# Rotation of queries and keys on GpSimd in a decoder layer's second projection pass, with twelve more expert dot products beside it

## What is computed

```python
def rope_partial(x, pos):                       # the first 16 of 64 columns of each head
    cos = jnp.cos(ang)[:, None, :]; sin = jnp.sin(ang)[:, None, :]
    x1, x2 = xr[..., :8], xr[..., 8:16]
    rot = jnp.concatenate([x1 * cos - x2 * sin, x2 * cos + x1 * sin], axis=-1)

def mix_projection(h, w_in, ln_g, ln_b, pos):   # h @ w_in -> u, vn, q, k, v
    q = rope_partial(q, pos) * (HEAD_DIM ** -0.5)
    k = rope_partial(k, pos)

# x += W_out [ gmlp_chunk(u, vn) || dilated window attention(q, k, v) ]
# x += peer_ffn(RMSNorm(x)):
    g = jax.nn.softmax(top_s, axis=-1)          # 8 heads x 16 experts of 16384 for each token
    hid = jax.nn.gelu(jnp.einsum('thkd,td->thk', u_tab[eid], xb))
    return jnp.einsum('thk,thkd->td', g * hid, v_tab[eid])
# y = RMSNorm(x)
```

## Time and profile before

| | us |
|---|---|
| median of 3 runs | 1731.89 |
| the runs | 1735.63, 1730.67, 1731.89 |
| span of the profiled execution | 1733.9 |

### The profile page before, as it was taken

One profiled execution on the slowest core, in us unless ns is written; L12 is line 12 of the kernel. 1 busy time (PEld: TensorE's weight loads), 2 busy tenths in 40 slices (PEclk: granted clock), 3 DMA queues, 4 the chain that ended last, 5 costly groups with the idle time before them and its releaser, 6 DMA issues.

```text
span 1733.9 us, 17751 instructions
## 1 busy us (share of the span) xinstructions
PE 1415.3 (82%) x5140; PEld 625.2 (36%) x5140; DVE 1086.9 (63%) x2913; ACT 637.0 (37%) x1905; POOL 654.3 (38%) x703
## 2 busy tenths in 40 slices
PE   6879997878998968888887887777777877777776
PEld 3475664444433333333332232222222322222211
DVE  2238987977200027777766666666667888888554
ACT  2421112455401004434444354444445434444443
POOL 3014434333366643333333333333333433333332
PEclk9889998788899988999999999999999999999999
DMA  9569899999999989999999999999999999999997
GB/s 342 201 263 336 311 325 349 390 395 408 394 366 351 387 322 372 413 418 402 401 421 410 421 410 422 421 421 412 414 415 411 406 422 414 405 421 418 409 391 325
DMA packets 111856, 664.80 MB, mean 383 GB/s; under 512 B 12912, under 2 KB 14176, under 8 KB 52240
## 3 DMA queue, kind: packets, MB, share of 16 engines
q0 software_dynamic: 97824, 571.75, 82.2%
q1 hardware_dynamic: 13936, 91.92, 13.5%
HBM read 658.02 MB, written 5.60 MB: 383 GB/s over the span
## 4 chain that ended last, share of the span: by engine, by line
DMA 37%; PE 31%; issue 10%; DVE 9%; ACT 8%; another core or an unknown queue 4%; POOL 0%; SPq 0%; ACTq 0%; DVEq 0%; POOLq 0%
DMA area_r<-in_uv_tab,eid 35%; PE bank L822 11%; PE bank L586 6%; PE bank L716 4%; ACT area_c L923 3%; PE bank L766 3%; PE bank L811 3%; DVE area_r L1563 2%; DMA area_w<-in_w_in 1%; PE bank L529 1%; DVE area_r L1554 1%; DVE area_x L1571 1%; PE bank L675 1%; ACT L1150 1%
## 5 line engine op out<-in xcount | busy, mean ns | idle before, releaser
L822 PE MATMUL bank<-area_r,area_c 128*128 128x512 f32 (+1 forms) x1584 | 776.6, 621 | 217.0 <-ACT area_c L923 211.4
L1726 POOL DMA_INDIRECT area_r<-in_uv_tab,eid x544 | 516.5, 949 | 967.3 <-PE bank L822 593.1
L1563 DVE CUSTOM_DVE_ANT_0 area_r<-area_r,bank 128x1024 f32<-128x1024 f32 x416 | 506.1, 1217 | 288.5 <-DMA area_r<-in_uv_tab,eid 287.8
L822 PEld LDWEIGHTS bank<-area_r,area_c 128*128 128x128 f32 (+1 forms) x1584 | 271.8, 187 | 715.4 <-issue 714.8
L1150 ACT ACTIVATE area_c<-hid 128x1 f32<-128x1 f32 x416 | 84.1, 202 | 539.4 <-DVE hid L1563 538.8
L1554 DVE CUSTOM_DVE_ANT_0 area_r<-area_r,bank 128x1024 f32<-128x1024 f32 x128 | 153.2, 1212 | 26.5 <-DMA area_r<-in_uv_tab,eid 26.0
L586 PE MATMUL bank<-area_w,area_t 128*128 128x384 f32 (+1 forms) x448 | 157.2, 507 | 6.2 <-DMA area_w<-in_w_in 5.6
L923 ACT ACTIVATE area_c<-ident,area_c 128x128 f32<-128x128 f32 x364 | 146.1, 401 | 34.8 <-PE bank L822 1.1
L1726 POOL DMA_INDIRECT area_r<-in_uv_tab,eidT x128 | 122.3, 955 | 92.2 <-issue 30.5
L766 PE MATMUL bank<-area_t,area_w 128*128 128x128 f32 (+1 forms) x512 | 129.6, 410 | 8.6 <-ACT area_x L923 7.9
L923 ACT ACTIVATE area_x<-bank 128x384 f32<-128x384 f32 (+8 forms) x125 | 50.3, 424 | 206.2 <-remote 65.5
(11 more groups left out here) (180 smaller groups left out, 1185.2 us busy)
## 6 DMA issues: line engine op xcount, KB each, us to landing
area_w<-in_w_in SPq DMA_DIRECT2D x12, 1536.0 KB, 8.9
area_w<-in_w_q SPq DMA_DIRECT2D x16, 1024.0 KB, 6.8
area_w<-in_k_cache SPq DMA_DIRECT2D x8, 1920.0 KB
area_r<-in_uv_tab,eid POOLq DMA_INDIRECT x544
area_w<-in_w_out SPq DMA_DIRECT2D x4, 2048.0 KB, 12.5
area_w<-in_v_cache SPq DMA_DIRECT2D x4, 1920.0 KB
area_v<-in_v_cache SPq DMA_DIRECT2D x4, 1152.0 KB
area_w<-in_w_in SPq DMA_DIRECT2D x2, 2048.0 KB, 12.7
```

What stands on the lines that cost most here:

```text
L822: mm = pe.matmul(acc[0:n, c, :], diag[by_pe(i) % DG][:, 0:n], x_ring[s][:, D + c * 512:D + (c + 1) * 512], start=(i == 0), stop=False, ski ...
L1563: vec.tensor_tensor_reduce(out=u, in0=u, in1=x_cur, scale=1.0, scalar=0.0, op0=ALU.mult, op1=ALU.add, accum_out=hid[t % 2][:, j:j + 1]).th ...
L1726: nc.gpsimd.indirect_dma_start(out=ring[s], out_offset=None, in_=table, in_offset=bass.IndirectOffsetOnAxis(ap=where, axis=0)).then_inc(la ...
```

## The change

In the second pass GpSimd does the rotations, with the same four operations; the first pass's stay on VectorE. GpSimd's queue is written out by unit: ahead of the rotation of unit u stand the fetches of tile 0 that `gathers_before(u)` allows. These are those whose slots are set free by the dot products made through unit u - 1, so dot products so far plus six, and no more than 16 for each head whose indices are made by then. The rotation waits for `proj_read` and, between its products and its sum, for a semaphore of its own (`rope_scaled`). 88 instead of 76 dot products stand ahead of and beside the pass, and a query or key unit weighs 8 instead of 6 in spreading them.

```diff
-DOTS_FIRST, DOTS_PROJ = 12, 76
+DOTS_FIRST, DOTS_PROJ = 12, 88
+        rope_scaled = sem("rope_scaled")
-        ROOM = [1 if t == SAMP else {"uv": 10, "q": 6, "k": 6, "v": 8}[CHUNKS[c][0]] for c, t in UNITS[NC:]]
+        ROOM = [1 if t == SAMP else {"uv": 10, "q": 8, "k": 8, "v": 8}[CHUNKS[c][0]] for c, t in UNITS[NC:]]
...
-                if UNITS[u] in qk_at:
-                    rotate(qk_at[UNITS[u]], u)
...
-            for i in range(U_END[0]):
+            def rotate(i, u):
+                c, t = QK[i]
+                n = TILES[t][1]
+                nh = HALF // HD
+                pool.wait_ge(proj_read, u + 1)
+                src = q_stage[i % 3] if CHUNKS[c][0] == "q" else k_stage[k_at[c, t]]
+                xr = src[0:n, :].rearrange("p (h d) -> p h d", d=HD)
...
+                nc.gpsimd.tensor_tensor(ab[:, 0], xr[:, :, 0:16],
+                                        rope[0:n, 32 * t:32 * t + 16].unsqueeze(1).to_broadcast([n, nh, 16]), ALU.mult)
+                nc.gpsimd.tensor_tensor(ab[:, 1, :, 0:8], xr[:, :, 8:16], cs[:, 2].to_broadcast([n, nh, 8]), ALU.mult)
+                nc.gpsimd.tensor_tensor(ab[:, 1, :, 8:16], xr[:, :, 0:8], cs[:, 3].to_broadcast([n, nh, 8]),
+                                        ALU.mult).then_inc(rope_scaled, 1)
+                pool.wait_ge(rope_scaled, i - NQ0 + 1)
+                nc.gpsimd.tensor_tensor(xr[:, :, 0:16], ab[:, 0], ab[:, 1], ALU.add).then_inc(roped, 1)
+
+            def gathers_before(u):
+                dots = dots_by_unit(u - 1)
+                heads = 2 + sum(dots >= dots_by_unit(NC + k - 1) + LINKS // 2 for k in ROUTE_PROJ)
+                return min(dots + UR, heads * TOPK)
+
+            issued = 0
+            for u in range(NC, len(UNITS)):
+                if UNITS[u] in qk_at:
+                    for i in range(issued, gathers_before(u)):
+                        gather_u(i)
+                    issued = max(issued, gathers_before(u))
+                    rotate(qk_at[UNITS[u]], u)
+            for i in range(issued, U_END[0]):
                 gather_u(i)
```

More of the change, by code:

```diff
@@ L1758, in gather_both @@
                 gather(x_ring, x_slot(i), uv_tab, eid[:, a:a + 1], x_landed)
-            for i in range(U_END[0]):
+            def rotate(i, u):
[5 more added lines that the diff above has]
+                xr = src[0:n, :].rearrange("p (h d) -> p h d", d=HD)
+                ab = rope_ab[0:n, (i % 2) * 192:(i % 2) * 192 + 192].rearrange("p (a h d) -> p a h d", a=2, h=nh)
+                cs = rope[0:n, 32 * t:32 * t + 32].rearrange("p (a o d) -> p a o d", a=4, o=1)
+                nc.gpsimd.tensor_tensor(ab[:, 0], xr[:, :, 0:16],
[17 more added lines that the diff above has]
+            for i in range(issued, U_END[0]):
                 gather_u(i)
```

## The result

The changed kernel takes 1745.84 us (median of six runs, 1742.74 to 1749.9) where the kernel before took 1731.28 beside it: ratio 1.0078 [1.0055, 1.01], some 13.5 us slower by the ratio and 14.6 by the medians. The forecast was 1731.1 us in a range of 1722 to 1743: wrong, and on the other side. Repeated on two more chips the ratio was 1.0102 and 1.0098.

What follows compares the result with a forecast made beforehand. No engine was taken to bound the whole; TensorE was nearly full in the pass, transfers in attention. 3.7 us lost in the pass and 4.5 gained in attention made -0.8 us: 1731.1 us from a median of 1731.89, range 1722 to 1743.

Steps and rivals of the forecast that it cites:

- The rotation's price: GpSimd in the second pass: one rotation of four operations takes 1.3 us, so its queue needs 89 of 99 us.
- rival (a): Second pass: GpSimd becomes the bound if a rotation exceeds 1.9 us; slower, 1738 us or near 1757 us; chance 0.28.
- its sign of several waits of TensorE: Second pass, trace of after: several waits of TensorE on GpSimd would speak for GpSimd becoming the bound.
- The figure of the Trainium skill: GpSimd's rotation: scaled, 288 elements would be 0.63 us plus a dispatch for each of four operations; not used in the sum.
- TensorE in the pass: Unit 10 of the second pass: the rotated tile comes 3.7 us later and TensorE loses 3.7 us; no later rotation adds.
- VectorE covered: Pass before unit 20: VectorE's 2.7 us more work is covered by its 3.37 us idle time at `gate_u` of tile 4.
- rival (c): Pass: fetches land late, VectorE waits 2 to 4 us together, 1733 to 1735 us; shares the forecast's chance of 0.38.
- The late end passed on in full: End of the pass: TensorE's 3.7 us slip reaches the attention stage in full, despite 10.5 us before ScalarE's release.
- Rival (b): End of pass and attention: the stall absorbs the 3.7 us and attention gives 6 us; faster, 1726 us; chance 0.34.
- The gain in attention: Attention stage after 417 us: twelve dot products fewer gain 4.5 us, between 3.0 and 7.7 us.
- Rival (d): Pass: the twelve dot products could be made late if head 5's indices were not ready; given nothing.
- The rule of the skill that was weighed: Pass: VectorE instructions with two SBUF inputs and GpSimd ones reading SBUF exclude each other; routing operations meet it, dot products not.

Runs made afterwards that it cites:

- the run with 76: Kernel before with GpSimd doing the rotations, dot products left at 76 and unit weights as before; ratio 1.0011 to the kernel before.
- the rotations earlier: Changed kernel (88 dot products) with three fetches less ahead of each rotation in GpSimd's queue; ratio 1.0083 to the kernel before.
- 82 and rotations earlier: Changed kernel with 82 instead of 88 dot products and three fetches less ahead of each rotation; ratio 0.9967, and 1.0011 the second time.
- the pause: Kernel before with one more wait on GpSimd: fetch 73 waits until ScalarE has read unit 27; it cost 0.23%.
- head 6's indices early: Changed kernel, head 6's routing moved into the pass (1.0052), begun in attention's group 0 with doubled steps (1.0034), or put ahead of attention's groups (ratio not given).
- the run with 82: Changed kernel with 82 instead of 88 of tile 0's dot products beside the pass, rotations on GpSimd; ratio 0.9983 [0.9968, 0.9998].
- both cures: Changed kernel (88), three fetches less ahead of each rotation, head 6's routing begun in attention's group 0 with two steps where it had one; ratio 1.0072.

## Why the prediction was wrong, point by point

**The rotation's price: right.** GpSimd's order of time shows the steps of one rotation; from 180.79 to the fetch at 182.29 it is 1.50 us, from the first start to the end of the last (181.75 + 0.39) 1.35, where 1.3 was taken:

```profile
180.79 0.39 POOL L1768 TENSOR_TENSOR area_c<-area_x,area_c 128x96 f32<-128x96 f32 x1
181.14 0.29 POOL L1770 TENSOR_TENSOR area_c<-area_x,area_c 128x48 f32<-128x48 f32 x1
181.39 0.28 POOL L1771 TENSOR_TENSOR area_c<-area_x,area_c 128x48 f32<-128x48 f32 x1
181.75 0.39 POOL L1774 TENSOR_TENSOR area_x<-area_c 128x96 f32<-128x96 f32 x1
182.29 0.97 POOL L1725 DMA_INDIRECT area_r<-in_uv_tab,eid  x1
```

GpSimd did not become the bound of the pass (63.45 of 99 us), and the rotation by itself changes nothing that can be told, as the run with 76 shows. So rival (a) did not happen as it was put, though the time came out on its side, and so did its sign of several waits of TensorE: for 16 us GpSimd was the bound (next point).
The figure of the Trainium skill (GPSIMD Engine Reference, section 3.1) had given 0.63 us for the elements plus four dispatches; the trace has 1.35. By that figure more than half of the time is not the elements', an estimate; the wait for `rope_scaled` is in it.

**TensorE in the pass: the first step that failed.** The forecast took one place, unit 10, and found 3.7 us; the trace has 3.68 us there. But two more places lose, units 5 and 7, and the working asked only whether units behind unit 10 add. Its own sum would not have found them: it puts the rotation of unit 7 at 4.6 us later (four more dot products, three rotations fewer, 2.1 us of queue), and the kernel before had 5.6 us of slack there:

```profile
192.60 0.25 DVE L1326 TENSOR_TENSOR area_x<-area_c 32x96 f32<-32x96 f32 x1
198.42 0.37 PE L529 MATMUL bank<-ident,area_x 32*128 32x32 f32 x3
```

The sum has the rotation wait for a dot product. In the trace it waits for GpSimd's own work and for a row: from 179.74 to 195.89 us GpSimd makes ten fetches and three rotations, and none of the fetches waits for a dot product. VectorE then runs out of rows. That of the next line was fetched at 187.46, six fetches before the one at 198.10; VectorE could begin on it 9.1 us later, and the fetch and the rotation of unit 7 are held behind it:

```profile
196.60 1.22 DVE L1555 CUSTOM_DVE_ANT_0 area_r<-area_r,bank 128x1024 f32<-128x1024 f32 x1 [3.97 <-DMA area_r<-in_uv_tab,eid]
...
198.10 1.07 POOL L1725 DMA_INDIRECT area_r<-in_uv_tab,eid  x1 [2.21 <-DVE hid L1555]
...
200.44 0.47 POOL L1774 TENSOR_TENSOR area_x<-area_c 32x96 f32<-32x96 f32 x1
```

In the two repeats VectorE waits 3.82 and 3.48 us (the latter in two pieces) there, and TensorE 2.48 and 2.22. The sum of TensorE's waits is 6.58 us, not 3.7. The second part of the failure has no term in the forecast at all: TensorE's granted clock falls to about half behind the waits of 2.40 and 3.68 us (the 0.50 us left it as it was), and the sixteen matmuls behind them cost 1.8 and 2.3 us more. Each of the two is thus dearer than the wait itself by three fifths and more: 2.40 + 1.76 and 3.68 + 2.26. With the rotations earlier, the sixteen behind waits of 1.50 and 1.82 us took 5.33 and 5.43 us, as without a wait.

**VectorE covered: the second step that failed.** `gate_u` of tile 4 still waits, 4.26 us, but only since TensorE came later still. VectorE reaches it at 250.65 us before (254.02 less 3.37) and at 261.82 after (266.08 less 4.26), 11.2 us later where 2.7 were worked out; in the repeats it is 11.7 and 12.9, and 10.7 with the rotations earlier. Busy time of that stretch, before and after (columns as in the earlier trace rows):

```profile
155.00:250.65 95.65, 95.32 (x517) 57.79 (x516) 90.05 (x281) 17.08 (x48) 40.15 (x43) 1.00 0.86 300
...
155.00:261.82 106.82, 99.07 (x513) 59.55 (x512) 93.63 (x241) 17.19 (x48) 69.82 (x113) 0.95 0.89 320
```

3.6 us are work. The other 7.6 are idle time, 6.6 of it waits for rows, of which the kernel before had none there: the transfers, costed at nothing, and rows that land late, called 2 to 4 us in rival (c). The cover of 3.37 us was thus spent whatever TensorE did. With TensorE's waits halved, VectorE alone brings the zeroing 7.2 us later, so a forecast with those waits at nothing would have been wrong too. Over the whole way to the zeroing the waits for rows are 9.6 us in the trace of after and 3.5 in that of before.

**The late end passed on in full: right, but by another path.** The time between TensorE's last projection and its reading hid none of the loss: 10.5 us before, 9.7 after (start +12.1 us in the mean of three pairs). Rival (b) fell with this. But the release does not follow TensorE. With the rotations earlier the last projection is 3.1 us later than before and the release 7.9 us; with 82 and rotations earlier they are 0.4 later and 1.2 earlier. In all eleven traces with the late reading the release comes 1.4 to 1.9 us behind the end of the last of a row of fetches, and a fetch can start only when VectorE's dot products have set its slot free. So TensorE's delay reaches attention over `gate_u` of tile 4 and VectorE.

**The gain in attention: the third step that failed.** 4.5 us were forecast for twelve; the three pairs have a length 0.6 us greater in the mean. With 82 the length is 150.2 us on the slower kind of chip, where four runs with 76 have 151.9 to 156.0 (mean 154.2), and 148.8 to 150.2 on the faster (five runs, mean 149.3), where the one run with 76, that with the pause, has 153.6: some 4 us for the first six. The second six bring nothing more. With 88 and head 6's indices early the length is 153.0 and 150.8 on the slower kind, 150.8 and 150.3 on the faster.

**Rival (d): the cause that was named and given nothing.** The forecast asked about head 5 and looked only at `ROUTE_PROJ`. The head that meets the new order is 6, in `ROUTE_ATT`. With its indices missing, five runs with 88, all on the slower kind, have a length of 151.1 to 158.2, mean 154.3: the kernel before's. That is 2.4 us over the mean of the two with the indices early. But the ranges overlap, the one pair on one chip differs by 0.3 us, and an idle time of 11 us cost nothing with 82. So in the traces this term is between nothing and 2 to 3 us, and I first read 7.6 us into it, from the lag of the cache loads. The medians of that one pair differ by 10 us, which no trace explains; why twelve gained nothing stays open.

**The sum again.** 12.1 us at the start of attention (mean of three pairs) and +0.6 in its length make 12.7 us at the first v row. The forecast had -0.8: 3.7 us in the pass, where 12.1 were lost, and 4.5 gained, where 0.6 were lost. The three ratios make 13.5, 17.7 and 17.0 us (0.0078, 0.0102 and 0.0098 of some 1733). The remaining 1 to 5 us stay open: the stage of v rows varies by 5 us from one execution to the next, and there is one profile for each median.

**The rule of the skill that was weighed.** VectorE's `L1423`, a `tensor_tensor` on 256 elements, takes 0.42 us in the kernel before; once, beside a rotation, it took 0.73, and the rotation's second step 0.48 instead of 0.29:

```profile
231.03 0.73 DVE L1423 TENSOR_TENSOR area_w<-rt 128x256 f32<-128x256 f32 x1
...
231.42 0.48 POOL L1770 TENSOR_TENSOR area_c<-area_x,area_c 128x48 f32<-128x48 f32 x1
```

By the Trainium skill (SBUF — State Buffer, "Who interferes with whom") a VectorE instruction with two SBUF inputs and a GpSimd instruction that reads SBUF exclude each other; the trace is in line with that, at 0.3 us for the meeting. It is the longest of the forty `L1423` of this trace, the median being 0.42 us; other meetings were not looked for. The dot products, with one input in PSUM, keep their mean of 1213 ns.

## What to carry to other kernels

When a step is moved behind another queue, work out its delay for every consumer, not for the tightest one alone, and follow the queue through the stretches where it never waits: there it is the bound, though its mean share is low. Add the clock that a longer wait can cost. Before a cover of a few microseconds is counted on, ask for the time at which each engine reaches it, waits for rows included. Take the change in halves: here half of it ran level with the kernel before, and the whole lost 0.8 to 1.0%. When a queue runs further ahead, follow it to the next thing it needs (here head 6's indices), and delay that thing on purpose before giving its wait a price: with 82 an idle time of 11 us on an engine cost nothing.

## What the runs showed of the hardware

**A reading that comes late on one kind of chip.** In the kernel before, on the chips of 1731 to 1735 us, ScalarE reads TensorE's last projection 9.8 to 10.5 us after its recorded end, in three traces of three, and in the changed kernel 7.0 to 9.7 us after it. Earlier, at the first seven fetches, the same shows: GpSimd issues from 116.57 to 125.09 us, and ScalarE's wait ends 1.4 us after the last of them.

```profile
124.15 0.94 POOL L1726 DMA_INDIRECT area_r<-in_uv_tab,eid  x1 [0.30 <-issue]
...
126.51 0.38 ACT L923 ACTIVATE area_w<-bank 128x256 f32<-128x256 f32 x1 [7.55 <-remote]
```

On a chip of 1709 us (the run with 82), with the same row of seven fetches from 115.62 to 124.14, ScalarE reads every five microseconds, in step with TensorE:

```profile
117.30 0.39 ACT L924 ACTIVATE area_w<-bank 128x256 f32<-128x256 f32 x1 [4.27 <-PE bank L787]
122.29 0.38 ACT L924 ACTIVATE area_w<-bank 128x256 f32<-128x256 f32 x1 [4.27 <-PE bank L787]
127.28 0.38 ACT L924 ACTIVATE area_w<-bank 128x256 f32<-128x256 f32 x1 [4.27 <-PE bank L787]
```

On the slower kind the one run without the late reading is that with head 6's routing in the pass, where gaps of 2.00 and 1.87 us break the row of fetches around TensorE's end; there ScalarE reads at 297.42, 0.5 us after TensorE's recorded last matmuls began. So on that kind the reading goes with the end of the row of fetches. That the row holds it is argued and not shown: the pause that was to prove it ran on the other kind, gaps of 0.8 to 0.9 us in the row did not end it, and in the kernel before ScalarE read the unit before the last in step at 282.59, inside a fetch with gaps of 0.33 and 0.35 us on its two sides. A loss is there without it too: the run with 88 and both cures loses 0.72% on the faster kind.

**Fetches and small arithmetic on GpSimd.** A fetch in a row takes 0.94 us and the next starts 0.30 us later, with rotations between them as before. The four operations on 96 and 48 elements take 0.39 and 0.28 to 0.29 us, and start 0.25 to 0.36 us apart; halving the elements takes away about a quarter of the time.
